# Hybrid decoder step on Trainium2: attention rounds of two tiles in five PSUM banks, with projections and sample attention placed inside them

## What is computed

```python
def mem_attend(cq, mk, mv, q_norm):
    q = head_rms(cq.reshape(B, L, MEM_HEADS, MEM_HEAD_DIM), q_norm)
    s = jnp.einsum('blhd,bmhd->bhlm', q, mk.astype(F32)) * MEM_HEAD_DIM ** -0.5
    p = jax.nn.softmax(s, axis=-1)
    return jnp.einsum('bhlm,bmhd->blhd', p, mv.astype(F32)).reshape(B, L, MEM_WIDTH)

def layer(x, i, mk, mv, hg_s0, buf_k, buf_v):
    h = rmsnorm(x, norm_mix[i])
    p = h @ w_in                     # of the layer's kind
    tok = hgrn_branch(...) or swa_prompt(...) / swa_sample(...)
    mo = mem_attend(cq, mk, mv, mem_q_norm[i])
    x = x + jnp.concatenate([tok, mo], axis=-1) @ w_out[i]
    g, u = jnp.split(rmsnorm(x, norm_ffn[i]) @ w_ffn_in[i], 2, axis=-1)
    return x + (jax.nn.silu(g) * u) @ w_ffn_out[i]
```

## Time and profile before

| | |
|---|---|
| runs of the kernel | 3180.23, 3189.64, 3225.75 us (median 3189.64) |
| span of the profiled execution | 3211.0 us |
| PE busy | 3026.3 us, 94% |
| PEld busy | 2710.9 us, 84% |
| DVE, ACT, POOL busy | 40%, 20%, 20% |
| mean granted clock of PE | 0.908 of 2.4 GHz |

### The profile page before, as it was taken

How to read it: one execution, slowest core, us unless ns; L and a number is a source line. 1 busy time by engine, 2 the same in 40 slices (tenths; PEclk the granted TensorE clock), 3 DMA queues, 4 the chain that set the end, 5 groups by cost and what they waited for, 6 DMA issues and landing times.

```text
span 3211.0 us, 41707 instructions
## 1 busy us (share of the span) xinstructions
PE 3026.3 (94%) x16482; PEld 2710.9 (84%) x16482; DVE 1291.0 (40%) x2031; ACT 652.2 (20%) x1044; POOL 642.1 (20%) x322
## 2 busy tenths in 40 slices
PE   6999999998899999999979989999979999999999
PEld 5878888897799999999958778878759999999997
DVE  4214444434544444444463143242452444444444
ACT  4311112212311111111142113131332111111110
POOL 4002322222411221112141010000033112211220
PEclk8589999998899999999986796867689999999999
DMA  5011011111111121112102210001002111111111
GB/s 164 12 53 36 26 47 47 47 35 28 53 40 39 39 59 39 39 39 54 45 20 60 66 34 14 14 14 43 1 27 60 40 39 44 54 39 39 40 45 54
DMA packets 186022, 135.33 MB, mean 42 GB/s; under 512 B 19616, under 2 KB 175456, under 8 KB 185888
## 3 DMA queue, kind: packets, MB, share of 16 engines
q1 hardware_dynamic: 181760, 129.69, 14.4%
q10 hardware_dynamic: 4160, 4.19, 0.4%
HBM read 124.61 MB, written 11.27 MB: 42 GB/s over the span
## 4 chain that ended last, share of the span: by engine, by line
PE 79%; PEld 9%; DVE 4%; issue 2%; ACT 2%; POOL 1%; PEldq 1%; DMA 1%; SPq 0%; DVEq 0%; ACTq 0%
PE ps L1239 40%; PE ps L1276 21%; PEld ps L1239 4%; PE ps L1401 4%; PE ps L1428 4%; PE ps L1413 2%; PEld ps L1547 2%; PE ps L1497 1%; PEld ps L1276 1%; POOL w_lo L488 1%; PEldq L1256 1%; PEld ps L1265 1%; DVE x L844 1%; PE ps L1453 1%; DVE normed_gained L841 1%
## 5 line engine op out<-in xcount | busy, mean ns | idle before, releaser
L841 DVE TENSOR_TENSOR x<-x,ps 128x512 f32<-128x512 f32 (+1 forms) x882 | 604.5, 686 | 911.6 <-PE ps L1276 890.3
L488 POOL TENSOR_TENSOR w_lo<-w_raw,w_hi 128x1024 fp32r<-128x1024 f32 x194 | 466.4, 2425 | 2304.9 <-ACT w_hi L484 2304.9
L1239 PE MATMUL ps<-hT_hi,w_hi 128*128 128x352 f32 x2976 | 721.7, 331 | 10.9 <-POOL w_lo L488 7.4
L1239 PE MATMUL ps<-hT_lo,w_hi 128*128 128x352 f32 x2976 | 712.4, 328 | 0.3
L1239 PE MATMUL ps<-hT_hi,w_lo 128*128 128x352 f32 x2976 | 709.1, 326 | 0.0
L1239 PEld LDWEIGHTS ps<-hT_hi,w_hi 128*128 128x128 f32 x2976 | 523.9, 192 | 39.9 <-POOL w_lo L488 7.7
L1239 PEld LDWEIGHTS ps<-hT_lo,w_hi 128*128 128x128 f32 x2976 | 526.3, 192 | 30.5 <-issue 2.7
L1239 PEld LDWEIGHTS ps<-hT_hi,w_lo 128*128 128x128 f32 x2976 | 525.1, 191 | 25.2
L1276 PE MATMUL ps<-w_hi,m_hi 128*128 128x512 f32 (+1 forms) x1060 | 428.6, 404 | 12.0 <-DVE m_lo L841 7.5
L1276 PE MATMUL ps<-w_lo,m_hi 128*128 128x512 f32 (+1 forms) x1060 | 425.2, 401 | 0.0
L1276 PE MATMUL ps<-w_hi,m_lo 128*128 128x512 f32 (+1 forms) x1060 | 423.8, 400 | 0.0
(11 more groups left out here) (225 smaller groups left out, 2620.9 us busy)
## 6 DMA issues: line engine op xcount, KB each, us to landing
w_raw<-in_w_ffn_in_dram SPq DMA_DIRECT2D x176, 256.0 KB, 3.3
w_raw<-in_w_ffn_out_dram SPq DMA_DIRECT2D x88, 256.0 KB, 3.7
w_raw<-in_w_in_hgrn_dram SPq DMA_DIRECT2D x52, 256.0 KB, 4.6
w_raw<-in_w_out_dram SPq DMA_DIRECT2D x32, 256.0 KB, 3.9
w_raw<-in_w_in_swa_dram SPq DMA_DIRECT2D x24, 256.0 KB, 3.8
x<-in_x_prompt_dram SPq DMA_DIRECT2D x8, 512.0 KB, 9.6
w_raw<-in_w_mem_kv_dram SPq DMA_DIRECT2D x16, 256.0 KB, 5.6
cache<-in_cache_mem_k_dram SPq DMA_DIRECT2D x4, 1024.0 KB, 7.2
```

The lines of the kernel that those rows point to most:

```text
L488: nc.gpsimd.tensor_tensor(slot(1, s), raw[:, j3, :], slot(0, s).bitcast(F32), ALU.subtract).then_inc(w_lo, 1)
L841: return V_.tensor_tensor(out, a, b, op)
L1239: return mmul(ps[:, b0 + g, 0:TW], slot(a, s)[:, P * k:P * k + P], hT[b][:, k, TW * g:TW * g + TW], start=m < 3, stop=m >= 69)
```

## The change

1. *Rounds of two tiles.* A pair has 16 rounds and 20 steps. Scores have one bank each (banks 0 and 1 in turn), turned probabilities bank 2, rows and turned output share bank 3, sample scores bank 4; banks 5 to 7 are free for a feature projection or for the output projection (6 and 7). ScalarE alone copies turned probabilities.
2. *Output in portions.* The turned output goes straight from bank 3 to m_hi (ScalarE, prompt_hi) and m_lo (VectorE, prompt_lo), 256 columns at a time, in odd steps from 5 on; the rows of the step wait for it.
3. *Sample attention in portions inside the rounds*: keys of one batch in each of steps 4 to 11, their scores in the following step, the softmax in 12 to 14, the turn in 15 and 16, the rows in 17.
4. *Fills inside the rounds.* Memory pairs: the first feature projection in steps 0 to 7, the second in 11 to 16 (layer 0) or 12 to 17 (layer 1). Group pairs: the output projection of the pair *before* in steps 1 to 9 (two groups a step), then the two query projections of the next group in steps 11 to 14 and 17 to 19. Pair 0's outs stay behind it, in banks 0 and 1. Pair 4 has no feature projections, and its own outs stay in the norms.
5. *Between pair 1 and group 0*: first query projection, key sums, query sums, second query projection, value projection. The order of the weight jobs follows. Key norms are taken one projection at a time, the first inside pair 1 at step 12.
6. *Arena addresses* of several tiles move; the forget gate of head 0 is computed inside pair 0 (hgrn_forget).

The core of the diff (ScalarE and TensorE; VectorE's stream follows the same steps):

```diff
+B_SC, B_PT, B_RO, B_SS, B_F = 0, 2, 3, 4, 5
+ROUNDS, STEPS = 16, 20
+S_KT, S_SSC, S_SPT, S_SPV, S_SOUT = 4, 5, 15, 17, 18
...
+            def sample_turn(p, b, n):
+                wait(act, sT, p, f"kt{b}")
+                if b >= 2:
+                    wait(act, sT, p, f"sc{b - 2}")
+                A(kcT[:, b % 2, 0:256 * n], ps[:, B_PT, 0:256 * n], ACT.Copy, sA, p, f"kt{b}")
...
+            def pair(p, g, before, after=None):
+
+                for s in range(STEPS):
+                    before(s)
+                    if s >= 5 and s % 2:
+                        prompt_hi(p, (s - 5) // 2)
+                    if s == S_SOUT:
+                        sample_hi(p)
+                    if s == S_SSC + NB:
+                        sample_exp(p, None if g is None else col(S_SROW + g))
+                    if 2 <= s < ROUNDS + 2:
+                        prompt_turn(ROUNDS * p + s - 2)
+                    if s < ROUNDS:
+                        half, _, h2 = at_round(s)
+                        prompt_exp(ROUNDS * p + s, None if g is None else col(S_SINK + 3 * (2 * half + h2) + g))
+                    if S_KT <= s < S_KT + NB:
+                        sample_turn(p, s - S_KT, 2 if g is None else 1)
...
+                        def before(s, g=g, n0=n0, u=u):
+                            if g and s == 0:
+                                head_squares(u + 1, B_F)
+                                pump.upto(n0 + 2)
+                            if g and s == 3:
+                                query_std(u + 1, B_F)
+                            if g < QG - 1:
+                                if s == 11:
+                                    pump.upto(n0 + 4)
+                                if s == 15:
+                                    head_squares(u + 2, B_F)
+                                    pump.upto(n0 + 5)
+                                if s == 16:
+                                    query_std(u + 2, B_F)
...
+            def pair(p, window, fill):
+
+                for s in range(STEPS):
+                    r = ROUNDS * p + s
+                    if s >= 5 and s % 2:
+                        prompt_out(r - 4)
+                    if S_SSC <= s < S_SSC + NB:
+                        sample_scores(p, s - S_SSC, window)
+                    if s == S_SPV:
+                        sample_rows_mm(p, window)
+                    fill(s, 0)
+                    if 3 <= s < ROUNDS + 3:
+                        if s >= 5:
+                            wait(pe, oV, p, f"{(s - 5) // 2}")
+                        prompt_rows(r - 3, window)
+                    if 2 <= s < ROUNDS + 2:
+                        if S_KT + 1 <= s < S_KT + NB + 1:
+                            wait(pe, sA, p, f"kt{s - S_KT - 1}")
+                        if s == S_SPT + 1:
+                            wait(pe, sV, p, "pt")
+                        prompt_turn(r - 2)
+                    if s < ROUNDS:
+                        prompt_scores(r, window)
+                    fill(s, 1)
+                    if S_KT <= s < S_KT + NB:
+                        sample_keys(p, s - S_KT, 1 if window else 2)
+                    if s == S_SPT:
+                        sample_turn(p, window)
...
+                    def fill(s, z):
+                        if s < 8:
+                            feat(J, 0, B_F, hZ, (2 * s + z, 16))
+                        if s == 11 and z == 0:
+                            wait(pe, hF, 0, "k")
+                        if 11 <= s < 17:
+                            feat(J + 1, 1, B_F, hQ, (2 * (s - 11) + z, 12))
...
+                    feat(J, 0, 0, qP)
+                    key_sums(U_KEYS + 1)
+                    query_sums(U_Q, 0)
+                    wait(pe, qD, U_KEYS + 1, "std")
+                    feat(J + 1, 1, B_F, qP)
```

More of the change, by code:

```diff
@@ L929, in prompt_max, with head_gain, key_norm @@
-            def prompt_max(r, first, head):
-                buf, s = (prob, prob2)[r % 2], 20 * (r % 4)
+            def head_gain(u, b0, dst, gain):
+                wait(dve, qQ, u, "sq")
+                V_.tensor_scalar(three(dst), fm(b0), gain, None, ALU.mult).then_inc(qG.sem, 1)
+            def key_norm(u, dst):
+                wait(dve, qD, u, "std")
+                V_.reciprocal(sq[:, :], sq[:, :]).then_inc(qR.sem, 1)
+                wait(dve, qR, u, "rstd")
+                tt(dst, dst, sq[:, :]).then_inc(qN.sem, 1)
@@ L1027, in pair @@
[L1027 to L1041 removed]
+                    rr = slice(64 * h2, 64 * h2 + 64)
@@ new lines, in sample_keys @@
+            def sample_keys(p, b, n):
+                if b == 0:
+                    pe.wait_ge(side_in, 16 * [2, 12, 16, 16, 16][p])
+                wait(pe, aC, ROUNDS * p + S_KT + b - 2, "pt")
+                for half in range(2):
+                    for i in range(n):
+                        c0 = (b * n + i) * 256 + P * half
+                        o0 = P * n * half + P * i
+                        ins = nc.tensor.transpose(ps[:, B_PT, o0:o0 + P], cacheb[:, c0:c0 + P], ident)
+                ins.then_inc(sT.sem, 1)
@@ L1532, in hgrn_head @@
                 wait(pe, hV, h, "q")
[L1533 removed]
+                wait(pe, hF, h, "ks")
                 for i in range(NPT):
@@ L1754, in _ @@
+                        if g:
+                            wait(pe, qN, u, "n")
+                        pair(2 + g, True, fill)
+                        J += 4 if g < QG - 1 else 2
+                    wait(pe, oV, NPAIR - 1, "7")
+                    ffn(L, (OUT0[1] + QG, J, srcs))
                 last_out = (FOUT0[L] + NCH - 1, FFN0[L] + FFN_JOBS - 1, [(1, LAST_SLOT)])
```

720 lines of the change are left out of this document (383 added, 337 removed).

## The result

The changed kernel takes 3209.2 us (median of 20 runs, 3204.9 to 3219.1), the kernel before 3200.3 (20 runs, 3179.4 to 3225.8). The ratio is 1.0041, 95% interval 1.0021 to 1.0060: slower by about 13 us, within the 2% that count as no change, where the forecast was 12 us faster.

A forecast was written before the change was run, and what follows sets the result against it. It took TensorE at its low clock to bound the old rounds, and loops across engines to lengthen the new steps. Terms -2 + 6 - 23 - 29 + 36 = -12 us took 3189.6 to 3178 us; range 3070 to 3255.

The forecast's parts named there:

- The sum: All touched stages: loops across engines and a partly low clock, -12 us in total, to 3178 us; chance 0.35.
- the term for groups 0 and 1: Groups 0 and 1, with fills and outs inside the rounds: 141.5 us each, -29 us.
- sign named for the sum: Profile after: about 8 us in steps 5 to 12, named waits, gap over 10, last group over 125, clock 0.75 to 0.85.
- First pair and outs: First memory pair with its fills, and the outs behind it: 159.5 us, -2 us.
- the allowance for a low clock: First pair, steps 5 to 12: 8.2 us three times and 8.4 five times, above 6.95 computed at the high clock.
- Second pair: Second memory pair, with key sums and the step 12 reciprocal partly uncovered: 136 us, +6 us.
- Between: Between second pair and first group: outs move into the group, the reciprocal loses its cover: 77 us, -23 us.
- Group 2: Last group, taking in 26 us of outs, with bare steps after the fills: 134 us, +36 us.
- the slower side's mechanism: Rival, all stalled steps: the clock falls there, +43 us, 3233 us; chance 0.20.
- TensorE stays the bound at the high clock: Rival, all pairs: loops cost nothing if ScalarE and VectorE run ahead; -135 us, 3055 us; chance 0.13.
- the point of decision: Steps 5 to 12: under 6 us would decide for TensorE staying the bound at the high clock.
- always at 2.4 GHz: Rival, all pairs: loops as in the sum but always at the high clock; -74 us, 3116 us; chance 0.25.

The follow-up runs named there:

- e3: Changed kernel with TensorE issuing the second key half's feature ahead of the first query sums, between pair 1 and group 0; median 3191.2 us.
- e9: Kernel of four order edits (e1, e2, e3, e4), plus step 15's output copy ahead of squares and split, low part ahead of gain; 3154.2 us.
- a0: The changed kernel run and traced again, unaltered; 3209.1 us, 1.0068 of the kernel before.
- e5: Changed kernel with eight added 256-column matmuls in each filling of group 2, steps 10 to 19; 3202.0 us.
- e4: Changed kernel with the first of a group's two feature weight blocks split in step 10 instead of 11, groups 0 and 1; 3198.5 us.
- e8: e1, e2, e3 and e4 together, plus rows issued behind turn and scores, and VectorE's row scaling behind the maximum; 3121.0 us.
- e1: Changed kernel with VectorE making the low part ahead of the residual add in steps 5, 7 and 9 of the groups; 3189.7 us.
- e2: Changed kernel with TensorE issuing a step's sample scores behind its first filling and rows, in all five round loops; 3173.1 us.
- e12: Changed kernel with 32 added 256-column matmuls between the narrow query sums and sample-row matmuls in the tails of groups 0 and 1; 3220.4 us.
- e11: Changed kernel with 32 added 256-column matmuls ahead of the rows of step 15, groups 0 and 1; 3198.6 us.

## Why the prediction was off

The sum had -12 us, the trace's stages have +6.5. Of the 31 us between 3178 and 3209.2, the sum has 18.5 and the base 10.6 (the three runs' median lay below that of 20); 2 us stay open. The step that failed is the term for groups 0 and 1, 17.5 us too small. Every sign named for the sum came: steps 5 to 12 of the first pair took 7.8 us on average, TensorE stood there for k_cacheT and m_lo and at a group's first feature for w_lo, a gap of 12.65 us holds the reciprocal, the last group is over 125 us, and the pairs' clock is 0.81 on average. So the mechanism was right and its size was not. By its own steps:

1. *First pair and outs: 159.5 forecast, 152.8 measured (123.75 + 29.04).* The loop was right to the hundredth: 6.95 us computed for a filled step at the upper clock, 6.93 to 7.00 measured. (The pieces were a little off: 2.7 us from scores to sample scores for 2.9, 1.05 and 0.84 for 0.98 and 0.73.) What was too much is the allowance for a low clock: 3.7 us in steps 5 to 7, for which 8.2 stood instead of 6.95, and 2.8 in steps 8 to 12, where the clock did fall, to 0.50 and 0.56 in steps 10 and 11 (9.37 and 10.01 us). *Second pair: 136 forecast, 131.7 measured*; steps 5 to 8 ran at 1.00 there too, and steps 10 and 12 took 10.58 and 9.96 us at 0.62 and 0.59.
2. *Between: 77 forecast, 80.9 measured.* The lost cover of the reciprocal was named, a gap of 13.7 us in all; the trace has it (1847.97 to 1860.62, 12.65). The excess is the first query projection, 13.9 us for 11.7 because it starts at 0.50, and the query sums, 4.0 for 2.0, all at 0.50. e3 shows that it was the price of one order and not of the change.
3. *Groups 0 and 1: 283 forecast, 300.5 measured.* This is the term that failed. The clock allowance was right in steps 5 to 9 by luck (42 forecast, 43.1 measured): these ran at 1.00 throughout (2090 to 2140 us), and the 1.15 us of each odd step come from the add queued ahead of the low part, which I hadn't followed on VectorE. Step 11 came out nearly as worked out (11.5 forecast, 12.3 and 12.7). The miss is at the group's ends: steps 0, 1 and 15 to 19 together, 44.2 forecast, 49.4 measured in group 1 and 50.0 in group 0. Step 15 alone took 8.7 and 8.8 us where 11.5 stood for steps 15 and 16; its rows stand 3.3 us for a low part behind squares, split and gain, and e9, with these out of the way, has 6.2 and 7.0. And the query sums and sample rows run at 1.2 GHz where I had put most of steps 17 to 19 at 2.4: the clock is at 0.50 for 23.9 us from step 15 on. Then there are steps 2 to 4, 16 forecast, 17.1 and 19.4 measured.
4. *Group 2: 134 forecast, 141.8 measured*, 136.8 in a0. So 5.1 us of the miss are the steps in which the clock fell in that execution; what is left is the start, steps 2 to 4 with 19.2 us for 16. I had put the bare half down to the low clock, and the chains of a0 and e5 bear that out.

The result came near no change partly by luck: the pairs were forecast 11 us too long and the rest 29 us too short. One reading was wrong: the old rounds did leave 0.50, since the earlier trace rows shows work of such rounds at the upper clock.

The rivals: the slower side's mechanism, the clock falling in all stalled steps, is right for steps 10 to 12 of the memory pairs (up to 10.6 us, at 0.50 to 0.72 but for step 12 of the first) and wrong for the groups, its main place. In steps 5 to 9 of the groups TensorE stood 1.8 us a step on average, and this row of the changed kernel (PE alone) has the full clock through nearly six of them:

```profile
2090.00:2140.00 50.00, 39.35 (x233) 1.00 0.00 1
```

The Trainium skill's section on depth-cycling (TensorE: Matmul & The Clock Gate, "A second HAM failure mode: psum-queue depth-cycling") would have the clock oscillate there; in steps 5 to 9 of the groups it mostly didn't, and in four of them (group 2 of the changed kernel's first trace, of e3 and of e5, group 1 of e4) one or two steps were longer for it, the longest 11.49 instead of 7.96 us at a clock of 0.55. Why the same kernel has this in one execution and not in the next is open. "TensorE stays the bound at the high clock" was given 0.13 and was wrong for this kernel only by the order on the queues: e8 is that kernel, at 6.06 us a step where I had set the point of decision at 6. It reached 3121 us, near the 3116 of "always at 2.4 GHz" and not the 3055 of its own estimate. By its trace the first pair is 24 us over that estimate (122 for 98) and group 2 is 21 over (121 for 100), each with several steps at 0.50 to 0.83; groups 0 and 1, with their tails at 0.50, are 11 over together, and the second pair with what follows it 9.

What was computed right is the size of the loops, and from that a result near no change. The error was to take the order of instructions as given, and so the waits as the price of the change; 88 us of the changed kernel's time, by the medians of it and of e8, were the price of that order.

## What to carry to other kernels

When work is cut into smaller rounds, write the loop through all engines down once per kind of step, queue by queue, and for each wait ask what stands ahead of the waited-for instruction that it doesn't need. An instruction that waits for another engine belongs behind the work of its own engine that doesn't; here the moves of single calls in e1, e2 and e3 were worth 12 to 29 us each by their traces, and that of e8 made TensorE the bound. Whether a low clock is a cost is read from the chain of waits: it is one where TensorE's own work stands on it, as in the bare steps of group 2. And work added to raise the clock stands on the same chain: in e5 it took back what the clock gave.

## What the runs showed of the hardware

- The granted clock stayed at 0.50 for 30.00 us with a matmul in flight all the time, where for about 18 us of them matmuls of 256 columns alternated with ones of 2 and 8 columns (e12), and fell after 13.89 busy us of 14.00 (e11). What kept it there is open.
- It stayed at 1.00 through 50 us in which TensorE was busy for 39.35, with a stand in each step (group 1 of the changed kernel). In the same steps of group 2, in the same execution, it fell to 0.55 for a step of 11.48 us; a second execution had 1.00 there.
- A reciprocal of 128 x 1056 values on VectorE took 6.76 us where a product of the same size took 1.26: five times as long.
- Added matmuls of 256 columns, 160 of them, brought the clock of a stretch from 0.54 to 0.83 and changed its length by 2.1 us only (e5), since they took 17.7 us of the chain themselves.
